# Hybrid encoder layer on one core: residual and norm of tiles 5 to 9 on ScalarE and GpSimd, one more ranking round at tile step 9, and the first expert's rows gathered and split earlier

## The reference

```python
# end of the token mixer, for each row
out = einsum('bsd,de->bse', gate_a * ya + gate_b * yb, w_out)
x   = x + out                                     # residual
# the expert layer
hn  = rmsnorm(x, norm_ffn)
aff = softmax(einsum('td,de->te', hn, w_router))  # 16 experts
gate, idx = top_k(aff.T, cap)                     # each expert takes its best rows: 128 of the sample, 32 of the prompt
xe  = hn[idx]
hdn = silu(xe @ w_gate) * (xe @ w_up)
y   = zeros.at[idx].add((hdn @ w_down) * gate)    # gathered, computed, scattered back
x   = x + y
return rmsnorm(x, norm_final)
```

## Time and profile before

| | us |
|---|---|
| runs of the kernel | 2145.74 median of 3 (2141.43 to 2147.66) |
| the profiled execution's own time | 2137.29 |
| its span, first to last instruction | 2135.6 |
| merge, about | 1076 to 1363.3 |
| experts, from | 1364.4 to the end |
| PE busy | 2045.4 (96%) |
| DVE busy | 1312.8 (61%) |
| ACT busy | 895.3 (42%) |
| POOL busy | 590.4 (28%) |

### The profile page before, as it was taken

One profiled execution on the slowest core, in us unless ns is written; L12 is line 12 of the kernel. 1 busy time (PEld: TensorE's weight loads), 2 busy tenths in 40 slices (PEclk: granted clock), 3 DMA queues, 4 the chain that ended last, 5 costly groups with the idle time before them and its releaser, 6 DMA issues. The chain is left out here.

```text
span 2135.6 us, 41837 instructions
## 1 busy us (share of the span) xinstructions
PE 2045.4 (96%) x17730; PEld 1663.2 (78%) x17730; DVE 1312.8 (61%) x1512; ACT 895.3 (42%) x1255; POOL 590.4 (28%) x585
## 2 busy tenths in 40 slices
PE   7999999999999999989889999899999999999996
PEld 6778888999999997778846666677777777777774
DVE  6556312125677657845567679767666767666665
ACT  5564211011111107721264442465565556556655
POOL 0000000002579756945554222111111111111201
PEclk9999999999999999999999999999999999999998
DMA  4233322237778658879965433487787888788787
GB/s 151 67 91 102 105 96 102 71 95 237 229 215 240 194 170 264 241 190 292 280 224 164 157 110 135 168 306 300 284 314 288 303 297 324 279 305 312 290 292 278
DMA packets 206762, 457.27 MB, mean 214 GB/s; under 512 B 99153, under 2 KB 134097, under 8 KB 179473
## 3 DMA queue, kind: packets, MB, share of 16 engines
q1 hardware_dynamic: 167664, 386.21, 52.6%
q0 software_dynamic: 14592, 45.70, 7.4%
q10 hardware_dynamic: 24352, 23.21, 4.1%
HBM read 356.72 MB, written 102.24 MB: 215 GB/s over the span
## 5 line engine op out<-in xcount | busy, mean ns | idle before, releaser
L80 DVE TENSOR_TENSOR ex_w_rest<-weights,ex_w_rounded 128x2048 fp32r<-128x2048 f32 x154 | 347.3, 2289 | 118.1 <-ACT ex_w_rounded L3066 118.1
L3066 ACT CAST ex_w_rounded<-weights 128x2048 fp32r<-128x2048 f32 x154 | 287.0, 1907 | 14.5 <-PEq L50 14.5
L2961 PE MATMUL ex_s_acc<-ex_w_rounded,ex_xt 128*128 128x512 f32 x1024 | 288.1, 395 | 0.7 <-DVE ex_xt L80 0.7
L2961 PEld LDWEIGHTS ex_s_acc<-ex_w_rounded,ex_xt 128*128 128x128 f32 x1024 | 188.3, 188 | 50.2 <-issue 13.2
L2961 PE MATMUL ex_s_acc<-ex_w_rest,ex_xt 128*128 128x512 f32 x512 | 158.1, 390 | 0.0
L87 PE MATMUL ch_wide<-normed,ch_w_rounded 128*128 128x512 f32 x384 | 153.1, 399 | 0.5 <-DVE normed_rest L80 0.5
L2915 POOL DMA_INDIRECT ex_xs<-hn,rt_sample_idx x16 | 21.5, 1341 | 472.4 <-PE ex_s_acc L3006 450.1
L87 PE MATMUL ch_wide<-normed,ch_w_rest 128*128 128x512 f32 x384 | 151.9, 395 | 0.0
L87 PE MATMUL ch_wide<-normed_rest,ch_w_rounded 128*128 128x512 f32 x384 | 151.8, 395 | 0.0
L2961 PE MATMUL ex_y_acc<-ex_w_rounded,ex_ht 128*128 128x512 f32 x512 | 147.7, 399 | 1.0 <-DVE ex_ht L80 1.0
L87 PE MATMUL tk_acc<-tk_w_rounded_first,normed 128*128 128x336 f32 x400 | 127.1, 318 | 1.9 <-PEq L50 1.9
(11 more groups left out here) (443 smaller groups left out, 4509.9 us busy)
## 6 DMA issues: line engine op xcount, KB each, us to landing
weights<-in_w_expert SPq DMA_DIRECT2D x154, 1024.0 KB, 9.1
ex_weights<-in_w_expert SPq DMA_DIRECT2D x38, 1024.0 KB, 8.9
laq<-sc_laq ACTq DMA_DIRECT2D x40, 384.0 KB, 4.9
tk_w<-in_w_tok SPq DMA_DIRECT2D x10, 1344.0 KB, 7.3
ch_w<-in_w_ch SPq DMA_DIRECT2D x24, 512.0 KB, 4.5
sc_rows<-rows SPq DMA_DIRECT2D x40, 256.0 KB, 4.3
dl_kv<-qkv_tok SPq DMA_DIRECT2D x40, 256.0 KB, 6.3
dl_qk<-laq SPq DMA_DIRECT2D x20, 512.0 KB, 6.8
```

Source lines behind the costliest of these rows:

```text
L80: return dve.tensor_tensor(out, whole, rounded.bitcast(F32), ALU.subtract)
L2961: mm = pe.matmul(banks[:, b], x[:, k, x_part], w[:, i % SPLIT, kk, 512 * b:512 * b + 512], start=(k == 0 and x_part == 0 and w is w_hi), s ...
L3066: act.copy(w_hi[:, i % SPLIT], raw(i)).then_inc(w_rounded, 1)
```

## The change

It has three parts.

1. `BY_POOL` goes from 7 to 5, and the tests on `LAST_SAMPLE` become tests on `BY_POOL`. So for tiles 5 and 6 the sum of the gated halves and the residual move from DVE to POOL, with a copy out of PSUM on ACT, and for tiles 5, 6 and 7 the norm moves from DVE to POOL (multiplication by the weights) and ACT (scaling). POOL's work on tiles 5 and 6 is now written between its steps for tiles 8 and 9. SP's load of the next rows of `x` into a buffer also waits for ACT's squares, which use that buffer as scratch.
2. The table `LOW_AT_ONCE` puts two low rounds instead of one at the third place of step 9, so one round fewer is left between the two groups of high rounds at the end.
3. The first expert's gather is issued by POOL at the end of the merge, as soon as `rt_sample_idx` is written, into a buffer that lies over `mg_wo_rounded`. At the start of the experts its rows are rounded and split ahead of the second piece of weights, and `BUSY_GATHER` is 4 instead of 12.

```diff
-LOW_AT_ONCE = {9: (0, 0, 1, 2), 10: (1, 1, 2, 3)}
+LOW_AT_ONCE = {9: (0, 0, 2, 2), 10: (1, 1, 2, 3)}
...
+    def gather(self, pool, dr, rows, e):
+        pool.indirect_dma_start(out=rows[:], out_offset=None, in_=dr["hn"], in_offset=bass.IndirectOffsetOnAxis(ap=self.sample_idx[:, e:e + 1], axis=0)).then_inc(self.gathered, 16)
...
+        wo_at = next_place(nc)
         wo_rounded = sb("mg_wo_rounded", [P, KT, D], F32R)
+        routing.rows_at = wo_at + 2 * D * 4
+        first_rows = routing.rows = nc.alloc_sbuf_tensor_at("rt_rows", [CAP_S, D], F32, offset=routing.rows_at)
...
                         if t >= 2:
                             sp.wait_ge(S["x2"], 2 * (t - 1))
+                        if t - 2 >= BY_POOL:
+                            sp.wait_ge(S["sqx"], t - 1)
                         sp.dma_start(xin[:, t % 2], io["x"][t * P:t * P + P, :]).then_inc(x_loaded[t % 2], 16)
...
-                        if t > LAST_SAMPLE:
+                        if t >= BY_POOL:
                             if h == 0:
                                 pool.wait_ge(S["const"], 32)
                                 pool.wait_ge(S["hn_turned"], t - 1)
...
-                add_gated(BY_POOL)
-                for t in range(BY_POOL, NT):
-                    if t + 1 < NT:
-                        add_gated(t + 1)
+                for t in range(1, NT):
+                    if t - 4 >= BY_POOL - 1:
+                        add_gated(t - 3)
+                    if t - 4 >= BY_POOL:
+                        add_residual(t - 4)
+                    attended(t)
+                add_gated(NT - 3)
+                for t in range(BY_POOL + 1, NT):
                     add_residual(t)
+                    if t + 2 < NT:
+                        add_gated(t + 2)
+                for b in range(2):
+                    pool.wait_ge(hn_stored[b], 16 * NT // 2)
+                pool.wait_ge(S["out_done"], 2 * NT)
+                pool.wait_ge(S["sample_listed"], 1)
+                routing.gather(pool, dr, first_rows, 0)
...
-                        squares = xin if t > LAST_SAMPLE else hn
+                        squares = xin if t >= BY_POOL else hn
...
-                        if t > LAST_SAMPLE:
+                        if t >= BY_POOL:
                             act.wait_ge(S["rstd_x"], t + 1)
-                            act.wait_ge(S["weighed"], 2 * (t - LAST_SAMPLE))
+                            act.wait_ge(S["weighed"], 2 * (t - BY_POOL + 1))
                             act.activation(hn[:, b], hn[:, b], ACT.Copy, scale=st[b][:, 66:67]).then_inc(S["hn"], 1)
...
-                    if has(c - 4):
+                    if 0 <= c - 4 < BY_POOL:
                         normed(c - 4)
...
-                normed(LAST_SAMPLE)
...
-                dve.tensor_copy(routing.sample_idx[:], listed[:, 0:16])
+                dve.tensor_copy(routing.sample_idx[:], listed[:, 0:16]).then_inc(S["sample_listed"], 1)
...
-BY_POOL = NT - 3
-BUSY_NORMED, BUSY_COPY, BUSY_TURNED, BUSY_RANKS, BUSY_GATHER, BUSY_ROUNDED = 16, 4, 4, 16, 12, 8
+BY_POOL = NT - 5
+BUSY_NORMED, BUSY_COPY, BUSY_TURNED, BUSY_RANKS, BUSY_GATHER, BUSY_ROUNDED = 16, 4, 4, 16, 4, 8
...
-        xs = sb("ex_xs", [CAP_S, D])
+        kept = sb("ex_kept", [P, (routing.rows_at - next_place(nc)) // 4 + D])
+        xs = routing.rows
...
-                gather(0)
                 gather_prompt(0)
...
                 round_weights(0)
-                round_weights(1)
                 round_x(0)
-                for i in range(2, AHEAD):
+                for i in range(1, AHEAD):
                     round_weights(i)
...
                 split_weights(0)
-                split_weights(1)
                 rest_x(0)
-                for i in range(2, AHEAD):
+                for i in range(1, AHEAD):
                     split_weights(i)
```

More of the change, by code:

```diff
@@ L2075, in __init__ @@
         self.gain_p = sb("rt_gain_p", [QUARTERS * CAP_P, EXPERTS])
+        self.gathered = nc.alloc_semaphore("rt_gathered")
+    def gather(self, pool, dr, rows, e):
+        pool.indirect_dma_start(out=rows[:], out_offset=None, in_=dr["hn"], in_offset=bass.IndirectOffsetOnAxis(ap=self.sample_idx[:, e:e + 1], axis=0)).then_inc(self.gathered, 16)
 def phase_merge(nc, io, dr, ident, weights, weights_ready, rest_ready, load_rest, load_ahead, first_tile, routing, held_at):
@@ L2144, in phase_merge @@
             "sig", "on_turned", "on_t", "y_done", "ga", "gb", "mixed", "mix_turned", "mix_t", "mix_rest", "wo_rounded", "wo_used", "wo_rest_pool", "wo_rest_dve", "out_done", "out_copied", "x2", "sqx", "ln_x", "rstd_x", "hn", "hn_turned", "hn_t",
-            "padded", "folded", "quads", "quads_out", "weighed", "logits", "lmax", "lneg", "lexp", "lrec", "aff", "aff_turned", "aff_taken", "ranked", "low_ranked", "merge", "prompt_listed", "quartered", "listed", "const", "filled")}
+            "padded", "folded", "quads", "quads_out", "weighed", "logits", "lmax", "lneg", "lexp", "lrec", "aff", "aff_turned", "aff_taken", "ranked", "low_ranked", "merge", "prompt_listed", "sample_listed", "quartered", "listed", "const", "filled")}
         inputs = [sem(f"mg_inputs{b}") for b in range(2)]
@@ L2216, in split_output, with attended @@
                         rest(pool, wo_rest(k), wo_whole(k), wo_rounded[:, k]).then_inc(S["wo_rest_pool"], 1)
-                for t in range(1, NT):
+                def attended(t):
                     b = t % 2
@@ L2859, in phase_experts @@
         quarters = lambda t: t.rearrange("t (q c) -> (t q) c", q=QUARTERS)
-        gathered, prompt_gathered, scattered = sem("ex_gathered"), sem("ex_prompt_gathered"), sem("ex_scattered")
+        gathered = routing.gathered
+        prompt_gathered, scattered = sem("ex_prompt_gathered"), sem("ex_scattered")
         w_rounded, w_split = sem("ex_w_rounded_done"), sem("ex_w_split")
@@ L2912, in gather @@
                 def gather(e):
-                    if e >= 1:
-                        pool.wait_ge(x_turned, e)
-                    pool.indirect_dma_start(out=xs[:], out_offset=None, in_=dr["hn"], in_offset=bass.IndirectOffsetOnAxis(ap=sample_idx[:, e:e + 1], axis=0)).then_inc(gathered, 16)
+                    pool.wait_ge(x_turned, e)
+                    routing.gather(pool, dr, xs, e)
                 def gather_prompt(g):
```

## The result

| | before | changed |
|---|---|---|
| median, us | 2145.74 (2141.43 to 2148.68, 9 runs) | 2157.12 (2151.95 to 2163.56, 9 runs) |
| ratio | | 1.0062, 95% interval 1.0049 to 1.0076 |
| profiled execution's span, us | 2135.6 | 2153.7 |

The change makes the kernel slower by 0.6%, about 13 us by the ratio (11.4 us between the two medians), where I had forecast 1.8 us less. The median lies outside my range of 2137 to 2149.

What follows compares the result with a forecast made beforehand. PE, busy 96% of 2135.6 us, was taken as the bound. Terms 0.3+0.45-2.55 = -1.8 us took the median from 2145.74 to 2143.9 us; range 2137 to 2149.

Steps and rivals of the forecast that it cites:

- The merge, +0.3: Merge, steps 9 to 11: PE's waits for the gating, now behind ACT's scaling, make it end 0.3 us later.
- the 1.11 us wait of step 10: Merge, step 10: PE's wait for DVE's gating of tile 8, claimed to stay at 1.11 us.
- Step 10: DVE's list bounds it: Merge, step 10: DVE gains a round, loses two residual halves and a norm: -0.04 us, shift +0.13.
- The paths of steps 9 and 11: Merge: from a tile's last product over ACT and DVE's gating to PE's next half, +0.17 and +0.30 us later.
- DVE's idle time ahead of the reciprocal: End of the merge: DVE's wait for ACT, 3.21 us before, would only grow, without gain.
- The rival of the relieved DVE: Merge: the 1.11 us wait vanishes, steps 9 and 11 lose nothing, merge gains 1.1 us; time 2142.4, chance 0.20.
- The end of the merge, +0.45: Merge's end: POOL, issuing the gather, comes last to the barrier; with the merge's shift, experts start 0.75 us later.
- POOL reaches the barrier: Merge's end: POOL arrives at 1364.0, after a 1.07 us gather issue, against DVE's 1363.55.
- the gather holds the barrier: Merge's end: an issue of 2.96 us delays POOL, first product +0.1 to +1.1 us; time 2146.3, chance 0.12.
- The start of the experts, -2.55: Experts' start: rows land under the shortened warm-up, first product 6.3 us behind the block's start instead of 8.85.
- Behind the first product nothing waits anew: Experts, after the first product: later pieces of weights are split before PE wants them; no added time.
- both kernels need the same time from it to the end: Experts: expected sign in the new profile, equal time from the first product to the end.

Runs made afterwards that it cites:

- e2_layout_back: The change with the gathered rows placed 7072 instead of 8192 bytes into the weights, so every expert tile has its address of before; ratio 1.0012.
- e11_two_gathers: The change with expert tiles at their addresses of before and a second 128-row gather behind the first; last index to first product 14.18 us against 11.98.
- e3_late_gather: The change, its layout kept, with the first gather issued again at the experts' start and `BUSY_GATHER` back at 12; ratio 1.0047.

## Why the prediction was wrong

Term by term:

- **The merge, +0.3: measured -0.38.** I had shifts of +0.17, +0.13 and +0.30, with the 1.11 us wait of step 10 staying. Measured are waits of 0.30, 0.25 and 0.24, 0.79 in all, in the place of one of 1.28 by the same measure. The step that failed is "Step 10: DVE's list bounds it". I had that list at -0.04: a round more, two residual halves and a norm less, everything else as long as before. But tile 9's attention took 4.87 us instead of 6.37, where the added round had moved it. With these 1.50 us DVE was ready 0.36 us before ACT (its reciprocal at 1283.12 waited that long), and ACT's path bounds step 10 too. Had the 1.50 us stayed, DVE would by my estimate have come 1.50-0.36 = 1.14 us later, and PE's wait would have been 0.25+1.14 = 1.39 us, about as long as before, as I had it. The paths of steps 9 and 11 were well read (within 0.15 us), and so was DVE's idle time ahead of the reciprocal, which grew and brought nothing. The rival of the relieved DVE had the right sign and a third of the size, but neither its condition that steps 9 and 11 lose nothing nor its reason, the dropped work, held.
- **The end of the merge, +0.45: measured 5.73-1.20 = +4.53.** The issue took the 1.07 us that I had taken, not 2.96. But it started 0.9 us behind the sample indices (1366.41 against 1365.35+0.17), not 0.1; what it waited for in that time the trace does not show. Above all the step "POOL reaches the barrier" is wrong: POOL's arrival counts from the landing, 4.6 us after the issue. My rival "the gather holds the barrier" had the place but the wrong mechanism, a long issue; the Trainium skill's rule on the shared port (SBUF — State Buffer, "SBUF: two separate sides") had no part in it, since the issue was as short as any.
- **The start of the experts, -2.55: measured 6.21-8.85 = -2.64.** This is right in its steps: half clock under the turns, the first product 6.3 us behind the block's start (6.21). The landing no longer mattered, being over before the block began. The clock rose earlier behind the start than I had it (by 1376.5, so 4.2 us at most, not 5.2), and DVE's part of `ex_xt` ended last. In part that is luck: in `e2_layout_back` and `e11_two_gathers` the second `keep_busy` took 2.54 and 2.96 us, where it took 2.17 here, and ended last; the first product came 6.20 and 6.27 us behind the start, because the two ends lie that close together.
- **Behind the first product nothing waits anew: true, and the pace cost 12.9 us.** That "both kernels need the same time from it to the end" is the step that decided the result, and it failed. I had listed what would refute me, "if the experts' pace changes", but never asked what could change it. The diff replaces a tile of 4096 bytes by one of 5216 in a stack of tiles that are allocated one behind the other, and I priced its dead bytes at nothing without a word. That is the term that failed.

So the sum was -0.38+4.53-2.64+12.9 = +14.4 us instead of -1.8. Without the fourth term the change would have been +1.5 us and the time inside my range, though on the other side of zero than I had it, and by a barrier that I had wrong: `e2_layout_back` is that kernel, at 1.0012.

Of the other edits that I had at nothing, the order of the splits was worth nothing (`e3_late_gather`). POOL's gated sums and SP's wait were not run by themselves; in steps 9 to 11 PE has no wait but the three above.

## What to carry to other kernels

- Read a diff for addresses too. A tile that grows, shrinks or goes moves all that are allocated behind it; here the experts' 128x512 products depend on the distance between their two operands, and of the distances tried (0, 32, 64, 96 and 128 modulo 256 bytes) 0 is the fast one. Compare the median record of a line before and after before looking for waits.
- A gather issued by GpSimd ahead of a block's end is no prefetch in this kernel: the block ends when it has landed. Either it is issued early enough to land under other work, or behind the barrier, where the other engines have something to do meanwhile.
- When an engine is relieved, find what its wait was for. DVE is busy 13.7 us less (1312.8 to 1299.1 us on the two pages), and the merge got 0.4 us shorter. By the working above they came from tile 9's attention, which took 1.50 us less at its new place, and not from the work that DVE dropped, which the added round used up.

## What was not expected of the hardware

- **The distance between stationary and moving operand.** The experts' 128x512 products of fp32r (the type of the rounded and remaining parts) take a median of 389 ns a record at 0 modulo 256 bytes, 393 at 128 and 397 at 96; over 2304 products in 762 us that is 9.9 to 13.2 us. The merge's products do not follow it (393 and 395 ns at 0, 392 at 128). Products of 256 columns show no gain from distance 0 (283 ns against 281 at 128), and the prompt's products take a mean of 381 ns in both kernels, though their stationary tile moved by 1120 bytes too. The Trainium skill (SBUF — State Buffer, "Operand start alignment") says of its own rule on start addresses that it is about legality and not speed; these runs add a case where speed depends on addresses that are all legal.
- **The barrier behind an indirect DMA of GpSimd.** The engines started 1.7 us after the last packet, with one gather and with two.
- **The same gather's issue beside other work.** The prompt's gather took 2.96 us right behind the first gather at the start of the experts, 0.16 us after a long DVE split from SBUF had begun; in the changed kernel, alone at the block's start, it took 0.96. The gather ahead is not what makes it long: three later prompt gathers of the kernel before also stand 0.30 us behind another gather, but beside a DVE instruction that reads PSUM, and take 0.94 to 0.97 us. The split is what goes with it: the last gather into `ex_yp` took 3.06 us before, issued at 2085.88 behind a split that began at 2085.79, and 0.99 after the change, issued at 2103.56 ahead of a split that began at 2104.05.
- **DVE and POOL side by side.** DVE's 128x256 multiplications of tile 9's attention took 0.41 to 0.43 us or 1.47 to 1.51, the long ones all while POOL multiplied 128x512 tiles, and POOL's multiplication into `mg_on` took 1.54 us beside them before (line 2234) and 1.29 after (line 2243). So moving a piece of work by one round can be worth more than dropping a norm (1.20 us). No run separates the cause.
